# Start addresses of the moving operands: 160 instead of 96 modulo 256, beside weight tiles that stay at 96

## The chip, the cores and the metric

The program runs on one core of a Trainium2 chip. The metric is the device time of one execution in microseconds (us). A core has five engines: TensorE (PE; its weight loads are listed apart as PEld), VectorE (DVE), ScalarE (ACT), GpSimd (POOL) and SyncE (SP, which starts DMAs here).

## What is computed

Two transformer blocks in a row on one sequence of 1024 tokens by 1024 features, all in float32. The first block mixes tokens with three kinds of attention, reads a memory of 256 tokens, and ends with a gated feed-forward network. The second block has a pooling mixer (four groups of 512 features, each averaged over its own window of 2, 4, 8 or 16 tokens) and then a sliding-window attention. Cut to its skeleton:

```python
x = first_block(x, mem, ...)      # attention x3, cross attention, feed-forward, final norm
h = modulate(rmsnorm(x, norm_g[0]), shift, scale)
u, z = split(h @ a_w_in)          # pooling mixer
p = causal_multiscale_pool(u)     # per group: mean over a trailing window, minus u
y = einsum("gc,gcd->gd", p, a_w_group) * a_scale
x = x + gate * ((y * silu(z)) @ a_w_out)
kb, vb = shared_kv_blocks(x, ...)
x = x + gate * swa_sink_mixer(...)   # sliding-window attention
return rmsnorm(x, final_g)
```

Nearly all arithmetic is in dense products `h @ W`.

## The kernel before

**A product in three passes.** Each float32 operand is written as a high part and a low part of type float32r, and a product is the sum of three: high by high, low by high, high by low. `product` (line 681) does this for one strip of weights. The weights are the stationary operand, a slice of 128 by 128 of `split_hi` or `split_lo`; the activations are the moving operand, 128 partitions by 512 columns of `h_hi` and `h_lo` (normed stream), `act_hi` and `act_lo` (hidden layer), `sum_hi` and `sum_lo` (sums of halves), `p_hi`, `p_lo`, `p_lo_x`, `y_hi`, `y_lo` and `pool_sums` (pooling mixer), and some smaller ones. Lines 691, 692 and 694 are its three matmuls. In `product_values` (lines 704 to 706) the sides are changed: a slice of `h_hi` or `h_lo` is stationary and 512 columns of the split weights move. The program issues a weight load ahead of each matmul.

**Weights in strips.** SP loads strips of weights into `raw` (two slots). ACT or POOL rounds them into `split_hi`, POOL subtracts to get `split_lo`, and PE uses them. `split_hi` and `split_lo` have two slots each, so a split waits until PE has done with the slot's last strip.

**Where tiles lie.** `sb` takes the next free bytes of each partition, in the order of the program. `shared` gives a list of tiles the next free bytes one after the other and frees them at once, so that tiles of several `shared` lists lie over each other; padding tiles (`w11`, `w21` and so on) put a tile at a chosen distance. Worked out from the shapes and the order, in bytes of a partition: `raw` begins at 7008, `split_hi` at 15200, `split_lo` at 23392, `h_hi` at 31584, `h_lo` at 64352, `xT` at 97120, and the large shared region at 129888. All of these are 96 modulo 256. Since nearly all later tiles are whole multiples of 256 bytes long, nearly all moving operands start at 96 modulo 256, at each of their 512-column halves too (2048 bytes). I call an operand's start modulo 256 its place, and the difference of the moving operand's place and the weights' place their distance.

**The exception.** `pooled` and `trail` (lines 243 and 244) have rows of T + EDGE floats, EDGE being 16. `w21` and `w22` (2 * EDGE floats, 128 bytes, lines 238 and 241) step over the end of `trail`. So `pool_sums` and `p_lo` begin 128 bytes later than the rest, at place 224. `p_lo_x` (declared behind `w20`) holds other parts of the same low operand and lies at place 96. `pooled_low` (line 600) says which of them a product of the pooling mixer reads: from the second group on, pieces 0 and 1 read `p_lo_x` and pieces 2 and 3 read `p_lo`.

**The other tiles.** `cols`, `cf` (identity and ones), `cb` and the small tiles lie ahead of `raw`. In the attention stages, probabilities, keys, values and queries lie in the shared region; the transposes (line 838) have a piece of probabilities as stationary operand and the identity of `cf` as moving one; line 850 multiplies transposed probabilities (stationary) by values (moving); line 828 makes the scores.

**Order.** The engines run lists written out by hand with semaphores between them. Nothing in the order depends on addresses.

Of the kernel before, what the change touches and what calls it, by code (L numbers as in the profile page):

```python
# [30 lines left out]
F32 = mybir.dt.float32  # L31
F32R = mybir.dt.float32r
# [5 lines left out]
P = 128  # L38
D = 1024
T = 1024  # L40
# [57 lines left out]
EDGE = 16  # L98
# [34 lines left out]
def build(nc, dram, out):  # L133
    ctx = ExitStack()
    with ctx:
# [3 lines left out]
        def sb(name, shape, dt=F32):  # L139
            return ctx.enter_context(nc.sbuf_tensor(name, shape, dt))  # L140

        def shared(tensors):

            with ExitStack() as phase:
                return [phase.enter_context(nc.sbuf_tensor(n, s, d)) for n, s, d in tensors]
# [19 lines left out]
        raw = sb("raw", [P, 2, D])  # L165
        split_hi = sb("split_hi", [P, 2, 8, P], F32R)
        split_lo = sb("split_lo", [P, 2, 8, P], F32R)

        ident, ones = cf[:, C_ID:C_ID + P], cf[:, C_ONE:C_ONE + P]
        eps, eps_squared = cf[:, C_EPS:C_EPS + 1], cf[:, C_EPS + 1:C_EPS + 2]  # L170
# [4 lines left out]
        def col(name, i=0, n=1):  # L175
# [9 lines left out]
        _, p1, pt1 = shared([("mla_qkv", [P, 3 * HEADS, T], F32), ("p1", [P, 4, HALF], F32), ("pt1", [P, 4, HALF], F32)])  # L185
# [3 lines left out]
        _, swa_klo0, swa_bias, p3, pt3 = shared([("x_kept", [P, KEPT, T], F32), ("swa_klo0", [P, T], F32R),  # L189
                                                ("swa_bias", [P, SWA_HEADS, 2 * P], F32), ("p3", [P, 4, 2 * P], F32),  # L190
                                    ("pt3", [P, 4, 2 * P], F32)])
        fox_rows, = shared([("fox_rows", [P, QT, D], F32R)])
        _, memw_lo = shared([("w18", [P, 6, T], F32), ("memw_lo", [P, 2, 8, P], F32R)])
        _, p_lo_x = shared([("w20", [P, 6, T], F32), ("p_lo_x", [P, 2, T], F32R)])
# [9 lines left out]
        _, _, _, _, _, _, fox_norm = shared([  # L204
            ("v1", [P, HEADS, MEM], F32), ("v2", [P, 2, HALF], F32), ("v3", [P, QT, HALF], F32),
            ("v4", [P, HEADS, CHK_SPAN], F32), ("v5", [P, 2, T], BF16), ("v6", [P, T], F32), ("fox_norm", [P, 2, T], F32R)])
        _, _, _, _, _, _, _, _, fox_aug, fox_kr = shared([
            ("a1", [P, HEADS, MEM], F32), ("a2", [P, 2, HALF], F32), ("a3", [P, QT, HALF], F32),
            ("a4", [P, HEADS, CHK_SPAN], F32), ("a5", [P, 2, T], BF16), ("a6", [P, T], F32), ("a7", [P, T], F32), ("a8", [P, T], F32),
            ("fox_aug", [P, HEADS, T], BF16), ("fox_kr", [P, 2, T], F32R)])  # L210
# [6 lines left out]
        _, _, _, memw_hi = shared([  # L217
            ("u1", [P, HEADS, MEM], F32), ("u2", [P, 2, HALF], F32), ("u3", [P, QT, HALF], F32), ("memw_hi", [P, 2, 8, P], F32R)])
# [9 lines left out]
        _, last_hi, last_lo = shared([("w13", [P, 16, T], F32), ("last_hi", [P, HID, T], F32R), ("last_lo", [P, HID, T], F32R)])  # L228
# [2 lines left out]

        _, sq_ffn = shared([("w14", [P, 13, T], F32), ("sq_ffn", [P, T], F32)])
        (_, sq3, sq_sum3, sq4, sq_sum4, rms4) = shared([
            ("w11", [P, 10 * T + 2 * EDGE], F32), ("sq3", [P, T], F32), ("sq_sum3", [P, T], F32),
            ("sq4", [P, T], F32), ("sq_sum4", [P, T], F32), ("rms4", [P, T], F32)])
        _, rms_end = shared([("w15", [P, 20 * T + 2 * EDGE], F32), ("rms_end", [P, T], F32)])
        (p_hi, y_hi, y_lo, _, pool_sums, p_lo) = shared([
            ("p_hi", [P, 4, T], F32R), ("y_hi", [P, 2, T], F32R), ("y_lo", [P, 4, T], F32R), ("w21", [P, 2 * EDGE], F32),
            ("pool_sums", [P, 12, T], F32R), ("p_lo", [P, 2, T], F32R)])
        (last_pair, first_tmp, gates, _, sums_f32, last_tmp) = shared([  # L240
            ("last_pair", [P, 4, T], F32), ("first_tmp", [P, 2, T], F32), ("gates", [P, 4, T], F32), ("w22", [P, 2 * EDGE], F32),
            ("sums_f32", [P, 12, T], F32), ("last_tmp", [P, 2, T], F32)])
        pooled, = shared([("pooled", [P, 4, T + EDGE], F32)])
        _, trail = shared([("w23", [P, 8, T], F32), ("trail", [P, 2, T + EDGE], F32)])
        pool_form = small[:, :, :].rearrange("p a n -> p (a n)")
        _, pool_tmp = shared([("w16", [P, 4, T + EDGE], F32), ("pool_tmp", [P, 3, HALF], F32)])
        _, sq_kv, sq_sum_kv = shared([("w19", [P, 10 * T + 2 * EDGE], F32), ("sq_kv", [P, T], F32), ("sq_sum_kv", [P, T], F32)])
        (swa_stack, swa_q, swa_kv, swa_z, swa_khi, swa_v, osb3, swa_klo1) = shared([
            ("swa_stack", [P, 2, 2, T], F32R), ("swa_q", [P, 2, T], F32), ("swa_kv", [P, 2, T], F32),
            ("swa_z", [P, NK, T], F32), ("swa_khi", [P, 2, T], F32R),  # L250
# [2 lines left out]
        _, gated_early = shared([("w12", [P, 2, 2, T], F32R), ("gated_early", [P, 2, HALF], F32R)])  # L253
# [3385 lines left out]
```

## Time and profile before

| what | value |
|---|---|
| device time, median of 3 runs | 2434.67 us (2433.75 to 2435.26) |
| span of the profiled execution | 2430.9 us |
| PE busy | 2369.3 us, 97% of the span |
| matmuls, weight loads | 11802, 11810 |
| granted TensorE clock, mean | 0.993 |

The profile is one execution, with all engines' instructions. The page gives busy times by engine, a picture of the span in 40 slices, the chain of work that ended last, and the costliest groups of instructions. A matmul's duration in it reaches from its start to the modelled end of its last column, so that successive matmuls overlap; how fast they follow each other is read from their start times. The granted clock has two levels here, 1.2 and 2.4 GHz; 1.00 stands for 2.4.

### The profile page before, as it was taken

How to read it: one execution, taken by the hardware profiler on the slowest of the kernel's cores; microseconds unless marked ns; L12 is line 12 of the kernel's file. 1: busy time of each engine (PE TensorE's matmuls, PEld its weight loads, DVE VectorE, ACT ScalarE, POOL GpSimd, SP SyncE). 2: the span in 40 equal slices, each digit the busy share in tenths (PEclk: the TensorE clock that was granted, in tenths of full speed). 3: DMA queues.
4: the chain of work that ended last, by engine and by line, in shares of the span. 5: the costliest groups of instructions: out<-in, count | busy, mean ns of one | idle time of the engine just before them, and what ended most of it. 6: DMA issues, size and time to landing. Idle time of an engine off the chain costs nothing.

```text
span 2430.9 us, 32848 instructions
## 1 busy us (share of the span) xinstructions
PE 2369.3 (97%) x11802; PEld 1965.9 (81%) x11810; DVE 1510.0 (62%) x1909; ACT 833.6 (34%) x1588; POOL 1273.0 (52%) x724
## 2 busy tenths in 40 slices
PE   7999999999999999999999999999999899999998
PEld 6887788888877888888888878878788787888877
DVE  6725555634577688878887678763754766045555
ACT  4211555612443222222222433231232333055663
POOL 4433964143044666666668344673846633465523
PEclk9999999999999999999999999999999999999999
DMA  5511000021011333333332111121121113100023
GB/s 215 158 44 44 1 1 30 7 113 51 11 40 48 113 120 122 121 121 121 121 121 65 48 44 44 57 65 58 64 82 56 57 64 130 52 27 19 27 101 134
DMA packets 67271, 177.31 MB, mean 73 GB/s; under 512 B 6847, under 2 KB 13761, under 8 KB 65113
## 3 DMA queue, kind: packets, MB, share of 16 engines
q1 hardware_dynamic: 58344, 148.58, 18.1%
q10 hardware_dynamic: 8816, 27.25, 3.2%
q8 instruction: 70, 1.15, 0.2%
q14 instruction: 41, 0.33, 0.0%
HBM read 160.04 MB, written 15.72 MB: 72 GB/s over the span
## 4 chain that ended last, share of the span: by engine, by line
PE 82%; DVE 6%; issue 5%; POOL 4%; ACT 2%; DMA 1%; SPq 0%; DVEq 0%; POOLq 0%; ACTq 0%
PE ps L691 22%; PE ps L694 21%; PE ps L692 21%; PE ps L850 6%; PE ps L828 4%; PE ps L838 3%; POOL split_lo L1606 1%; DVE h_lo L565 1%; PE ps L705 1%; PE ps L704 1%; PE ps L706 1%; PE ps L487 1%; POOL small L1625 1%; DMA raw<-in_strips 1%; DVE h_lo L568 1%
## 5 line engine op out<-in xcount | busy, mean ns | idle before, releaser
L691 PE MATMUL ps<-h_hi,split_hi 128*128 128x512 f32 (+1 forms) x1576 | 628.7, 399 | 20.0 <-DVE h_lo L568 13.3
L692 PE MATMUL ps<-h_lo,split_hi 128*128 128x512 f32 (+1 forms) x1576 | 612.7, 389 | 0.0
L694 PE MATMUL ps<-h_hi,split_lo 128*128 128x512 f32 (+1 forms) x1576 | 548.3, 389 | 0.0
L1482 POOL TENSOR_TENSOR split_hi<-raw,cf 128x1024 fp32r<-128x1024 f32 x70 | 137.0, 1958 | 498.8 <-PE ps L694 393.5
L691 PEld LDWEIGHTS ps<-h_hi,split_hi 128*128 128x128 f32 x1576 | 298.0, 189 | 80.7 <-issue 12.2
L694 PEld LDWEIGHTS ps<-h_hi,split_lo 128*128 128x128 f32 x1576 | 297.3, 189 | 61.8
L692 PEld LDWEIGHTS ps<-h_lo,split_hi 128*128 128x128 f32 x1576 | 298.0, 189 | 56.1 <-issue 1.2
L1557 POOL TENSOR_TENSOR split_lo<-raw,split_hi 128x512 fp32r<-128x512 f32 x144 | 230.4, 1619 | 199.8 <-ACT split_hi L2495 199.5
L1606 POOL TENSOR_TENSOR split_lo<-raw,split_hi 128x512 fp32r<-128x512 f32 x96 | 148.7, 1558 | 170.8 <-ACT split_hi L2653 169.5
L1484 POOL TENSOR_TENSOR split_lo<-raw,split_hi 128x1024 fp32r<-128x1024 f32 x70 | 195.3, 2790 | 5.5
L2495 ACT CAST split_hi<-raw 128x512 fp32r<-128x512 f32 x144 | 86.8, 622 | 286.0 <-PE ps L694 214.0
L888 DVE CUSTOM_DVE_ANT_0 p<-ps,swa_bias 128x256 f32<-128x256 f32 (+1 forms) x128 | 52.2, 408 | 154.1 <-PE ps L828 152.9
L988 ACT COPY pt<-ps 128x256 f32<-128x256 f32 (+3 forms) x216 | 79.9, 370 | 180.9 <-PE ps L838 180.6
L838 PE MATMUL ps<-cf,p 128*128 128x128 f32 x712 | 122.2, 276 | 10.4 <-ACT p L980 6.8
L691 PE MATMUL ps<-act_hi,split_hi 128*128 128x512 f32 x320 | 125.4, 392 | 3.0 <-DVE xT L3131 2.9
L692 PE MATMUL ps<-act_lo,split_hi 128*128 128x512 f32 x320 | 124.5, 389 | 0.0
L2653 ACT CAST split_hi<-raw 128x512 fp32r<-128x512 f32 x96 | 58.7, 621 | 161.9 <-PE ps L694 155.8
L838 PEld LDWEIGHTS ps<-cf,p 128*128 128x128 f32 x712 | 86.8, 144 | 32.8 <-ACT p L980 19.3
L3131 DVE TENSOR_TENSOR xT<-xT,ps 128x1024 f32<-128x1024 f32 x72 | 87.4, 1214 | 31.0 <-PE ps L694 31.0
L3007 DVE SCALAR_TENSOR_TENSOR ada_acc<-ada_raw,cact,ada_acc 128x1024 f32<-128x1024 f32 x56 | 102.6, 1832 | 0.8
L691 PE MATMUL ps<-p_hi,split_hi 128*128 128x512 f32 x256 | 100.1, 391 | 1.5 <-DVE p_lo L3211 1.5
L692 PE MATMUL ps<-y_lo,split_hi 128*128 128x512 f32 x256 | 99.6, 389 | 0.0
(447 smaller groups left out, 5139.7 us busy)
## 6 DMA issues: line engine op xcount, KB each, us to landing
raw<-in_strips SPq DMA_DIRECT2D x208, 256.0 KB, 2.7
raw<-in_strips SPq DMA_DIRECT2D x86, 512.0 KB, 3.5
ada_raw<-in_ada SPq DMA_DIRECT2D x64, 512.0 KB, 3.8
memw_raw<-in_mem_strips SPq DMA_DIRECT2D x8, 512.0 KB, 6.3
xT<-in_xT ACTq DMA_DIRECT2D x4, 1024.0 KB, 7.9
x_spill_d<-xT ACTq DMA_DIRECT2D x1, 3584.0 KB, 9.9
xT<-x_spill_d ACTq DMA_DIRECT2D x2, 1792.0 KB, 11.0
out_T<-out_sb SPq DMA_DIRECT2D x14, 256.0 KB, 2.2
```

Source lines behind the costliest of these rows:

```text
L691: pe.matmul(acc[:, a:b], w_hi, hi[:, a:b], start=first, stop=False)
L692: pe.matmul(acc[:, a:b], w_hi, lo[:, a:b], start=False, stop=False)
L694: mm = pe.matmul(acc[:, a:b], w_lo, hi[:, a:b], start=False, stop=last)
L828: mm = pe.matmul(at[:, lo:hi], q, k, start=j == 0, stop=j == len(group) - 1)
L838: mm = pe.transpose(bank(4 + b % 2, P, j * P), probs[:, (b0 + j) * P:(b0 + j + 1) * P], ident)
L850: mm = pe.matmul(o, a["pt"][:, w % 4, j * P:(j + 1) * P], unit["values"][b0 + j], start=b0 + j == 0, stop=b0 + j == nblk - 1)
L1482: pool.tensor_tensor(hi, raw[:, r, :], ones[:, 0:1].to_broadcast([P, D]), ALU.mult).then_inc(hi_split, 1)
L1484: pool.tensor_tensor(lo, raw[:, r, :], rows(hi), ALU.subtract).then_inc(split_ready[r], 1)
L1557: pool.tensor_tensor(form_tiles(split_lo, p), src, rows(form_tiles(split_hi, p)), ALU.subtract).then_inc(form_ready, 1)
L1606: pool.tensor_tensor(group_tiles(split_lo, p), src, rows(group_tiles(split_hi, p)), ALU.subtract).then_inc(form_ready, 1)
L3007: dve.scalar_tensor_tensor(out=ada_acc[:, :], in0=ada_raw[:, r, :], scalar=cact[:, k:k + 1], in1=ada_acc[:, :], op0=ALU.mult, op1=ALU.add) ...
L3131: dve.tensor_tensor(xT[:, o, :], xT[:, o, :], pair(2 + o % 2), ALU.add).then_inc(ffn_res, 1)
```

## The change

A new tile `beside_weights` of 16 floats (64 bytes) is put behind `split_lo`. It is never used. All tiles behind it begin 64 bytes later: `h_hi`, `h_lo`, `xT` and the large shared region, and with them all moving operands of `product`, which go from place 96 to place 160. `raw`, `split_hi` and `split_lo` stay at 96. The paddings `w21` and `w22` grow from 128 to 256 bytes, and those of the tiles that lie over them likewise, so `pool_sums` and `p_lo` go from place 224 to 160 too. No instruction is added, removed or moved, and no order is changed.

```diff
         split_lo = sb("split_lo", [P, 2, 8, P], F32R)
+        sb("beside_weights", [P, 16])
...
-            ("w11", [P, 10 * T + 2 * EDGE], F32), ("sq3", [P, T], F32), ("sq_sum3", [P, T], F32),
+            ("w11", [P, 10 * T + 4 * EDGE], F32), ("sq3", [P, T], F32), ("sq_sum3", [P, T], F32),
...
-        _, rms_end = shared([("w15", [P, 20 * T + 2 * EDGE], F32), ("rms_end", [P, T], F32)])
+        _, rms_end = shared([("w15", [P, 20 * T + 4 * EDGE], F32), ("rms_end", [P, T], F32)])
...
-            ("p_hi", [P, 4, T], F32R), ("y_hi", [P, 2, T], F32R), ("y_lo", [P, 4, T], F32R), ("w21", [P, 2 * EDGE], F32),
+            ("p_hi", [P, 4, T], F32R), ("y_hi", [P, 2, T], F32R), ("y_lo", [P, 4, T], F32R), ("w21", [P, 4 * EDGE], F32),
             ("pool_sums", [P, 12, T], F32R), ("p_lo", [P, 2, T], F32R)])
...
-            ("last_pair", [P, 4, T], F32), ("first_tmp", [P, 2, T], F32), ("gates", [P, 4, T], F32), ("w22", [P, 2 * EDGE], F32),
+            ("last_pair", [P, 4, T], F32), ("first_tmp", [P, 2, T], F32), ("gates", [P, 4, T], F32), ("w22", [P, 4 * EDGE], F32),
             ("sums_f32", [P, 12, T], F32), ("last_tmp", [P, 2, T], F32)])
...
-        _, sq_kv, sq_sum_kv = shared([("w19", [P, 10 * T + 2 * EDGE], F32), ("sq_kv", [P, T], F32), ("sq_sum_kv", [P, T], F32)])
+        _, sq_kv, sq_sum_kv = shared([("w19", [P, 10 * T + 4 * EDGE], F32), ("sq_kv", [P, T], F32), ("sq_sum_kv", [P, T], F32)])
```

## Rows read from the trace of the kernel before

**Rows 1.** The page: span, engines' busy times, chain that ended last.

```profile
span 2430.9 us, 32848 instructions
...
PE 2369.3 (97%) x11802; PEld 1965.9 (81%) x11810; DVE 1510.0 (62%) x1909; ACT 833.6 (34%) x1588; POOL 1273.0 (52%) x724
...
PE 82%; DVE 6%; issue 5%; POOL 4%; ACT 2%; DMA 1%; SPq 0%; DVEq 0%; POOLq 0%; ACTq 0%
```

**Rows 2.** PE's groups, shapes apart: line, out<-moving,stationary, count | busy us, mean ns | idle.

```profile
L691 PE MATMUL ps<-h_hi,split_hi 128*128 128x512 f32 x1544 | 619.6, 401 | 20.0 <-DVE h_lo L568 13.3 <-DVE h_lo L565 4.7 <-DVE h_lo L2925 1.8
L692 PE MATMUL ps<-h_lo,split_hi 128*128 128x512 f32 x1544 | 603.6, 391 | 0.0
L694 PE MATMUL ps<-h_hi,split_lo 128*128 128x512 f32 x1544 | 539.2, 392 | 0.0
...
L692 PE MATMUL ps<-act_lo,split_hi 128*128 128x512 f32 x320 | 124.5, 389 | 0.0
...
L692 PE MATMUL ps<-y_lo,split_hi 128*128 128x512 f32 x256 | 99.6, 389 | 0.0
...
L691 PE MATMUL ps<-sum_hi,split_hi 128*128 128x512 f32 x240 | 94.4, 393 | 2.1 <-POOL split_lo L1557 2.1
...
L704 PE MATMUL ps<-split_hi,h_hi 128*128 128x512 f32 x64 | 24.9, 389 | 0.0
```

**Rows 3.** One tile's instructions, `p_lo` (224), then `p_lo_x` (96): durations min/median/max ns.

```profile
L692 PE MATMUL ps<-p_lo,split_hi x64: 391/395/395, 1486.6 to 1951.5; 128*128 128x512 f32 x64
...
L692 PE MATMUL ps<-p_lo_x,split_hi x48: 387/389/397, 1633.4 to 1948.7; 128*128 128x512 f32 x48
```

**Rows 4.** One tile's instructions, `pool_sums` (place 224): the three matmul lines.

```profile
L692 PE MATMUL ps<-pool_sums,split_hi x160: 387/393/628, 1483.9 to 1922.6; 128*128 128x512 f32 x160
...
L691 PE MATMUL ps<-pool_sums,split_hi x144: 390/395/792, 1555.5 to 1922.4; 128*128 128x512 f32 x144
...
L694 PE MATMUL ps<-pool_sums,split_lo x144: 390/396/628, 1556.0 to 1922.9; 128*128 128x512 f32 x144
```

**Rows 5.** Timeline of PE, moving operands at 96 only: start us, duration us, instruction.

```profile
1300.10 0.39 PE L691 MATMUL ps<-h_hi,split_hi 128*128 128x512 f32 x1
...
1329.80 0.39 PE L694 MATMUL ps<-sum_hi,split_lo 128*128 128x512 f32 x1
```

**Rows 6.** Timeline of PE, moving operands at 224 only.

```profile
1576.01 0.40 PE L694 MATMUL ps<-pool_sums,split_lo 128*128 128x512 f32 x1
1576.25 0.39 PE L691 MATMUL ps<-pool_sums,split_hi 128*128 128x512 f32 x1
1576.48 0.40 PE L692 MATMUL ps<-pool_sums,split_hi 128*128 128x512 f32 x1
...
1580.92 0.39 PE L694 MATMUL ps<-pool_sums,split_lo 128*128 128x512 f32 x1
```

**Rows 7.** Timeline of PE behind a stall, moving operands at 96.

```profile
1021.26 0.50 PE L691 MATMUL ps<-act_hi,split_hi 128*128 128x512 f32 x1 [0.55 <-DVE xT L3131]
1021.60 0.39 PE L692 MATMUL ps<-act_lo,split_hi 128*128 128x512 f32 x1
...
1022.76 0.39 PE L691 MATMUL ps<-act_hi,split_hi 128*128 128x512 f32 x1
```

**Rows 8.** Timeline of PE, scores of float32 operands, 256 columns each, no float32r.

```profile
611.37 1.02 PE L828 MATMUL ps<-mem_k,cross_q 128*128 128x256 f32 x4
```

**Rows 9.** Timeline of PE at the lower clock; then the groups of the transposes and values.

```profile
761.33 0.63 PE L694 MATMUL ps<-sum_hi,split_lo 128*128 128x512 f32 x1
...
763.46 0.63 PE L692 MATMUL ps<-sum_lo,split_hi 128*128 128x512 f32 x1
...
L838 PE MATMUL ps<-cf,p 128*128 128x128 f32 x712 | 122.2, 276 | 10.4 <-ACT p L980 6.8 <-DVE h_lo L944 2.8 <-DVE small L897 0.3
...
L850 PE MATMUL ps<-vbc,pt 128*128 128x64 f32 x528 | 68.4, 273 | 0.0
```

## What the change does to the time, forecast from these rows

> **What bounds the kernel now.** I read the page first. PE is busy 97% of the span, and the chain of work that ended last lies on PE for 82% of it [rows 1]; each of the three lines of `product` carries some 21 to 22% of the span there. So the kernel is a stream of matmuls, and what counts is how fast one follows the other. The change touches no instruction. It can move the time only if the rate of that stream depends on where the operands lie. So the next views are PE's groups by shape, the single tiles, and the timeline.
>
> In the groups the reader sees one size all over: 512 columns, 389 ns from start to modelled end [rows 2]. The starts tell more. From 1300.10 to 1329.80 us there are 131 matmuls whose moving operand is at place 96, and (1329.80 - 1300.10) / 131 = 226.7 ns from start to start [rows 5]. A duration of 389 ns so goes with a step of 227 ns, 162 ns less. At 2.4 GHz 512 columns take 213.3 ns, if one column goes in per cycle; at the lower clock, 1.2 GHz, (763.46 - 761.33) / 5 = 426 ns is just 512 / 1.2, with nothing on top [rows 9]. So at the higher clock each step has 13.4 ns that the columns don't explain.
>
> **The step does depend on the place.** The pooling mixer's tiles show it. `p_lo` is at 224 and `p_lo_x` at 96; they are pieces of the same operand, read by the same line in the same loop. Their medians are 395 and 389 ns [rows 3], 6 ns apart, and the two ranges (391 to 395; 387 to 397) are narrow. `pool_sums`, also at 224, has medians of 393, 395 and 396 ns [rows 4]. In its unbroken stream, (1580.92 - 1576.01) / 21 = 233.8 ns per step, with single steps of 0.24 and 0.23 us in turn [rows 6]. Against 226.7 that is 7.1 ns more. The weights are at 96 in all of these. So either a distance of 128 bytes to the weights costs 6 to 7 ns, or the place 224 by itself does; the trace can't part the two, as no weights of `product` lie elsewhere. It has no long matmul at place 160, or at a distance of 64, either.
>
> A third fact: at place 96 too the step isn't always 226.7. Behind a stall, five steps from 1021.60 to 1022.76 take 232 ns each [rows 7], before the stream falls into its steady step. So 226.7 is a favourable rhythm that place 96 finds, and some 232 to 234 ns is what it costs to be out of it.
>
> [...]
>
> **The change part by part.** First the tiles that go from 96 to 160. Their matmuls in `product` are: `h_hi` and `h_lo`, 3 x 1544; `act`, 3 x 320; `sum`, 3 x 240; `y_lo`, 256 [rows 2]. `p_hi` has another 512 and `y_hi` 256, and the small ones with `product_values` (3 x 64, where the weights' side moves instead) bring about 400. Together about 7,700. The price of one is unknown, so I bound it. From above, by the nearest rows at another place: 395 - 389 = 6 ns [rows 3], or 7.1 ns by the steady stream [rows 6]. From below, by the smallest excess of any stream in the trace: the scores of rows 8, with float32 operands, start every (1.02 - 0.38) / 3 = 213 to 215 ns (0.38 us being one such matmul's duration) for 256 columns at two cycles each, so nearly no excess. If all 13.4 ns but the 2 of that row were lost through place, a better place could give back 11 ns. So the bounds are -11 and +7 ns. I take +3 ns: the distance, 64 bytes, is halfway between the two that are known (0 costs nothing, 128 costs 6), and place 160 lies halfway between 96 and 224. It is a choice and not a reading. Sum: 7,700 x 3 = 23 us.
>
> Second, the tiles that go from 224 to 160: `pool_sums` 448 and `p_lo` 64 matmuls, 512 [rows 3, 4]. They pay 6 ns now and would pay 3: 512 x -3 = -1.5 us. If the new place were as good as 96, this would be -3 us.
>
> Third, the transposes, 712 with `cf` as the moving side [rows 9], and some 170 more of their kind. Their stationary side moves and the identity stays, so their distance goes from -32 to -96. [...] If each lost the 3 ns, 880 x 3 = 2.6 us, of which part lies beside waits for ACT; I put them at 0 to 2.6 us and take 1. The values (line 850), keys and queries: both sides move by 64, distance as before, nothing from the distance. The other engines' instructions read and write whole rows as before; their durations in the trace don't bear on places, and they have idle time beside PE (DVE 62%, POOL 52% busy [rows 1]), so 0, with up to 1 us either way. DMAs to tiles: `raw` stays; those to `xT` and `ada_raw` are hidden but for the first, 0.
>
> **What of it lies on the path.** PE is idle for 2430.9 - 2369.3 = 61.6 us in all [rows 1], where it waits for splits or norms. Where POOL or ACT end such a wait, slower matmuls just shorten it. The chain has 82% on PE and 5% in issue, and most of the rest is waits that begin with a PE result and so move along. I take 90%: 0.9 x (23 - 1.5 + 1) = 20 us. The sum against the profiled execution: 2430.9 + 20 = 2451; the median of the runs is 3.8 us above the span, so about 2455 us.
>
> **Rivals.**
> 1. *As bad as 224 (slower, in full).* If what counts is which half of 256 bytes a stream begins in, 160 and 224 are alike. Then 7,700 x 6 x 0.9 = 42 us: 2476. For it: 224 is the only other place that is known, and the stream behind a stall also runs at 232 to 234 [rows 6, 7]. Against it: nothing. I treat it as the upper part of my slower case.
> 2. *Nothing happens at 160 (no change).* The good rhythm holds over a window of distances and only 128 falls out. Then the 512 pooled matmuls go from 395 to 389 and 3 us are gained, less if their waits take it up: 2432. For it: 96 and its rhythm are a broad, steady state that returns within some six steps after each stall. Here also belongs the case that place matters for no reason that 64 bytes touch. [...]
> 3. *A better place (faster).* The 13.4 ns are themselves a cost of streams that start at the same place as the weights, and 64 bytes apart they don't meet. The price is per matmul of `product`, and it decides as soon as the step at 160 is under about 226 ns. With half of the 11 ns back: 8,200 x 5.5 = 45 us, or 2390; with all of it 90 us, or 2345. For it: the excess isn't there at 1.2 GHz, nor with float32 operands [rows 8, 9], so it isn't a fixed cost of a matmul. Against it: 0 is the better of the two distances that are known, and the step is the same to 0.1 ns for all 96-tiles, which looks like a floor.
>
> [...]
>
> **How the numbers follow.** A measurement of this kernel can tell about 0.2%, 4.9 us, from no change. Slower by more: 0.46, of which rival 1 takes about half. Within 0.2%: 0.20, rival 2 and small prices. Faster by more: 0.34, rival 3. The likeliest is the slower case, and its time is 2455, its own range 2440 to 2480. The range reaches from half of rival 3's gain, 2385, to rival 1 with a little more, 2482; outside are the full gain of rival 3 and prices above 7 ns, together under 0.2.
>
> **What would show each step.** In the profile after, `h_lo` and `act_lo` on line 692 have a mean duration of 392 ns by my sum (389 now), 395 by rival 1, 389 by rival 2, under 385 by rival 3. An unbroken stream of `h` and `sum` matmuls steps by 230, 233, 227 or under 222 ns. `p_lo` and `p_lo_x` must come out alike, whatever the price; if they don't, place modulo 256 isn't what counts. If the steps stay at 227 and the time moves nevertheless, the cause is outside PE and the whole argument is wrong. The prediction is wrong in its main choice if a place between two known ones isn't between them in price.

## The result: 0.5% slower, and the profile after

The changed kernel takes 2447.85 us (median of 4 runs, 2446.37 to 2449.15) against 2434.97 us of the kernel before on the same chip (4 runs). The ratio is 1.0048, with a 95% interval of 1.0036 to 1.006. The profiled execution's span is 2445.3 us, 14.4 us above that of before.

The page after, its lines that answer to [rows 1]:

```profile
span 2445.3 us, 32848 instructions
...
PE 2382.5 (97%) x11802; PEld 1966.9 (80%) x11810; DVE 1512.1 (62%) x1909; ACT 832.7 (34%) x1588; POOL 1275.5 (52%) x724
...
PE 84%; DVE 7%; issue 4%; POOL 3%; ACT 2%; DMA 1%; SPq 0%; DVEq 0%; POOLq 0%; ACTq 0%
```

The instruction counts are the same. PE is busy 13.2 us longer and idle 62.8 us instead of 61.6, so nearly all of the 14.4 us lies in the stream of matmuls. The other engines' busy times move by at most 2.5 us.

PE's groups after, with shapes apart (lines are one higher, because of the new line of code), answering to [rows 2]:

```profile
L693 PE MATMUL ps<-h_lo,split_hi 128*128 128x512 f32 x1544 | 606.1, 393 | 0.0
...
L693 PE MATMUL ps<-act_lo,split_hi 128*128 128x512 f32 x320 | 125.2, 391 | 0.0
...
L693 PE MATMUL ps<-y_lo,split_hi 128*128 128x512 f32 x256 | 99.9, 390 | 0.0
...
L705 PE MATMUL ps<-split_hi,h_hi 128*128 128x512 f32 x64 | 25.2, 394 | 0.0
```

The mean durations rise by 1 to 2 ns in `product` (`h_lo` 391 to 393, `act_lo` 389 to 391, `y_lo` 389 to 390) and by 5 ns in `product_values` (389 to 394). The single tiles, answering to [rows 3] and [rows 4] (durations min/median/max):

```profile
L693 PE MATMUL ps<-p_lo,split_hi x64: 388/392/394, 1499.4 to 1964.7; 128*128 128x512 f32 x64
```

```profile
L693 PE MATMUL ps<-p_lo_x,split_hi x48: 387/390/397, 1644.4 to 1961.9; 128*128 128x512 f32 x48
```

```profile
L692 PE MATMUL ps<-pool_sums,split_hi x144: 388/392/793, 1568.1 to 1935.3; 128*128 128x512 f32 x144
...
L695 PE MATMUL ps<-pool_sums,split_lo x144: 388/392/628, 1568.6 to 1935.7; 128*128 128x512 f32 x144
```

`p_lo` comes down from 395 to 392 ns and `pool_sums` from 395 and 396 to 392. `p_lo_x`, which left place 96, goes up by 1. Now that all of them are at place 160 they are nearly alike, as they should be if the address modulo 256 is what counts.

The timeline shows the step itself. First a stream of `h` alone, as in [rows 5] (start us, duration us):

```profile
520.28 0.39 PE L692 MATMUL ps<-h_hi,split_hi 128*128 128x512 f32 x1
520.51 0.39 PE L693 MATMUL ps<-h_lo,split_hi 128*128 128x512 f32 x1
520.74 0.39 PE L692 MATMUL ps<-h_hi,split_hi 128*128 128x512 f32 x1
520.97 0.39 PE L693 MATMUL ps<-h_lo,split_hi 128*128 128x512 f32 x1
521.19 0.62 PE L695 MATMUL ps<-h_hi,split_lo 128*128 128x512 f32 x2
```

Successive steps are no longer all 226.7 ns. Read in ns they run 226, 229, 232 and again; from 503.80 to 529.89 us there are 114 steps of 228.9 ns on average. The steady rhythm of [rows 5] is gone, but not the whole price of [rows 6] is paid.

Then a place where this profile holds its own control. Up to 114.11 us `memw` weights and `mem` activations are multiplied; both lie behind the new tile, so both moved and their distance is still 0. From there on line 705 has `h` as stationary side, at 160, and the split weights, at 96, as moving one: distance -64.

```profile
109.81 0.39 PE L707 MATMUL ps<-memw_hi,mem_lo 128*128 128x512 f32 x1
...
113.66 0.39 PE L706 MATMUL ps<-memw_lo,mem_hi 128*128 128x512 f32 x1
113.89 0.39 PE L707 MATMUL ps<-memw_hi,mem_lo 128*128 128x512 f32 x1
114.11 0.39 PE L705 MATMUL ps<-split_hi,h_hi 128*128 128x512 f32 x1
114.35 0.39 PE L706 MATMUL ps<-split_lo,h_hi 128*128 128x512 f32 x1
...
118.78 0.39 PE L707 MATMUL ps<-split_hi,h_lo 128*128 128x512 f32 x1
```

The 19 steps up to 114.11 take (114.11 - 109.81) / 19 = 226 ns, and the 20 steps after it (118.78 - 114.11) / 20 = 233.5 ns. The lines, the shape and the order stay the same across that point, with no idle time; the tiles change, and with them places and distance. Before the change the second group ran like this:

```profile
112.46 0.39 PE L704 MATMUL ps<-split_hi,h_hi 128*128 128x512 f32 x1
...
115.86 0.39 PE L704 MATMUL ps<-split_hi,h_hi 128*128 128x512 f32 x1
```

That is 15 steps of 226.7 ns. Its moving side, the split weights, is at 96 in both kernels, and it lost 6.7 ns all the same; the first group went from 96 to 160 and lost nothing. Both point at the distance and not at the moving operand's place.

Then a stage where the change costs nothing. The sliding-window scores, before and then after (first and last start):

```profile
L828 PE MATMUL ps<-swa_khi,swa_stack x128: 220/364/365, 2130.7 to 2333.1; 128*128 128x256 f32 x112, 128*128 128x128 f32 x16
```

```profile
L829 PE MATMUL ps<-swa_khi,swa_stack x128: 222/364/368, 2143.6 to 2346.0; 128*128 128x256 f32 x112, 128*128 128x128 f32 x16
```

They begin 12.9 us late and end 12.9 us late. In this stage the `product` matmuls come three at a time between others. Where one follows another here, the step was already 229 ns on average before the change and is 229 ns after it: the steady rhythm was never reached, and there was none to lose.

### The profile page after: what moved, and what is told of

Same layout as the page of the kernel before. It is cut to its first block, busy times and chain, and to the rows that moved or that the text cites. A ratio compares the mean times of both kernels' runs of the same rounds, so it can differ in the third digit from the quotient of the medians.

```text
span 2445.3 us, 32848 instructions
## 1 busy us (share of the span) xinstructions
PE 2382.5 (97%) x11802; PEld 1966.9 (80%) x11810; DVE 1512.1 (62%) x1909; ACT 832.7 (34%) x1588; POOL 1275.5 (52%) x724
## 4 chain that ended last, share of the span: by engine, by line
PE 84%; DVE 7%; issue 4%; POOL 3%; ACT 2%; DMA 1%; SPq 0%; DVEq 0%; POOLq 0%; ACTq 0%
PE ps L692 22%; PE ps L695 22%; PE ps L693 22%; PE ps L851 6%; PE ps L829 4%; PE ps L839 3%; POOL split_lo L1607 1%; DVE trail L3228 1%; DVE h_lo L566 1%; PE ps L705 1%; PE ps L707 1%; PE ps L706 1%; PE ps L488 1%; DVE h_lo L569 1%; ACT p L981 0%
```

## The experiments

The question after the result: is it the distance between weights and moving operand that sets the step, or the moving operand's own place? And what does the curve look like? In all kernels below but e9 the paddings `w21` and `w22` have 256 bytes, so that all moving operands of `product` share one place.

### e1: the pooled tiles alone

```diff
-            ("p_hi", ...), ("w21", [P, 2 * EDGE], F32),
+            ("p_hi", ...), ("w21", [P, 4 * EDGE], F32),
```

and the other paddings likewise; no `beside_weights`.

> Only the paddings w21 and w22 (and those over them) grow to 256 bytes; beside_weights is left out. Every moving operand of product, pool_sums and p_lo included, is then at place 96, the weights stay at 96. Theory of the distance and theory of the place agree: 512 matmuls go from 393 to 396 ns down to 389, 3 us less, 2432 us (2429 to 2435). If p_lo stays at 395 ns, something other than address modulo 256 makes these tiles slow.

Measured: 2435.44 us against 2435.56, ratio 1.0001 (0.9992 to 1.001). The matmuls did what both theories say:

```profile
L692 PE MATMUL ps<-p_lo,split_hi x64: 389/389/389, 1489.7 to 1956.1; 128*128 128x512 f32 x64
```

All 64 are at 389 ns, from 395 in [rows 3]. The time didn't follow. The expected gain, 3 us or 0.13%, is just outside the interval. The first and last start of `p_lo` were 464.9 us apart before and are 466.4 here. In e2, e7 and e8 below, where `p_lo` is at distance 0 too, they are 467.6, 463.3 and 463.3 apart. So single executions differ by more than the 3 us that are sought. Matched one by one with those of the kernel before, the 512-column steps without a wait, at the higher clock, take 3.2 us less in e1's trace, but PE's idle time is 64.7 us instead of 61.6. Why it waits longer isn't shown.

### e2: everything 64 bytes later, weights too

```diff
+        sb("ahead_of_weights", [P, 16])
         fox_raw, = shared([("fox_raw", [P, 2, T], F32R)])
```

> The 64 bytes are put ahead of raw instead of behind split_lo, with the larger w21 and w22: weights and moving operands all at place 160, distance 0. Theory A (the distance between weights and moving operand counts): the steady step is 226.7 ns again and the time that of e1, about 2432 us. Theory B (the place of the moving operand counts): place 160 costs as in the changed kernel, steps of 226 to 232 ns, about 2448 us.

Measured: 2436.13 us, ratio 1.0001 (0.9991 to 1.0011). The timeline:

```profile
507.65 0.39 PE L693 MATMUL ps<-h_lo,split_hi 128*128 128x512 f32 x1
...
533.94 0.39 PE L693 MATMUL ps<-h_lo,split_hi 128*128 128x512 f32 x1
```

116 steps, 226.6 ns each. The moving operands are at place 160, just as in the changed kernel, and nothing is lost. The theory of the place falls.

### e3: weights 64 bytes later, moving operands at 96

```diff
+        sb("ahead_of_weights", [P, 16])
         fox_raw, = shared([("fox_raw", [P, 2, T], F32R)])
...
         split_lo = sb("split_lo", [P, 2, 8, P], F32R)
+        sb("beside_weights", [P, 48])
```

> 64 bytes ahead of raw and 192 behind split_lo: weights at place 160, all moving operands at 96, distance -64 (192 modulo 256). Theory A: product costs what lines 705 to 707 cost in the changed kernel, where the distance is -64 and the step 233.3 ns: 7,700 x 6.6 x 0.9 = 46 us more, about 2480 us. Theory B: moving operands are at 96 as before, about 2432 us; only product_values, whose moving side is the weights at 160, changes.

Measured: 2466.94 us, ratio 1.0133 (1.0118 to 1.0149).

```profile
507.76 0.39 PE L693 MATMUL ps<-h_hi,split_hi 128*128 128x512 f32 x1
...
533.90 0.39 PE L693 MATMUL ps<-h_hi,split_hi 128*128 128x512 f32 x1
```

112 steps, 233.4 ns each, though the moving operands are where they were before the change. The distance it is. The step came out as forecast, the time 13 us lower: less than 0.9 of the steps' price reaches the end. The sign counts too: 64 bytes one way cost 2.2 ns, the other way 6.7. The same trace has the mirror image, which the changed kernel has the other way round. In `product_values` the split weights move, so here the distance is +64 where `product` has -64:

```profile
115.01 0.39 PE L706 MATMUL ps<-split_hi,h_hi 128*128 128x512 f32 x1
...
118.90 0.39 PE L708 MATMUL ps<-split_hi,h_lo 128*128 128x512 f32 x1
```

These 17 steps take (118.90 - 115.01) / 17 = 228.8 ns, against 233.4 in `product`. So what counts is the moving operand's start minus the stationary one's, whichever of the two holds the weights.

### e4 to e8, e11, e12: the curve

These differ in the size of `beside_weights` alone (e7: none, but 40 floats ahead of the weights).

```diff
-        sb("beside_weights", [P, 16])
+        sb("beside_weights", [P, 32])
```

> beside_weights has 32 floats (128 bytes) instead of 16: weights at 96, all moving operands of product at 224, distance 128. Theories A and B agree on this one: all of them cost what pool_sums and p_lo cost before, 232.4 to 233.8 ns per step, so 7,700 x 6 x 0.9 = 42 us more, about 2476 us. It tells whether the price of the 512 pooled matmuls holds for all.

> beside_weights has 8 floats: distance 32 bytes, moving operands of product at place 128. If the price rises evenly with the distance from 0 (0: 226.7 ns, 64: 229.0, 128: 232.4), the step is some 228 ns and the time 7,700 x 1.2 x 0.9 = 8 us above before, about 2443 us. Rival: the price is low inside a window around 0 and 32 still falls into the steady rhythm of 226.7 ns: about 2435 us. Rival: a distance just off 0 is better than 0 (the 13 ns above the columns' 213.3 are themselves a cost of meeting): steps of 216 to 224 ns, 2360 to 2420 us.

> beside_weights has 56 floats: distance 224, that is -32 modulo 256; moving operands at place 64. If the curve is even on both sides of 0 it is like e5. If it climbs again to 0 only at the end (192: 233.5), the step is some 230 ns and the time about 2455 us. A step under 226 ns would speak for a best distance other than 0.

> 160 bytes ahead of raw: weights and moving operands all at place 0, distance 0, starts at whole multiples of 256. Theory of the distance alone: 226.7 ns per step, 2435 us as before. Rival: the 13.3 ns above the columns are the price of operands that don't start at a multiple of 128 bytes (17 pieces of 128 bytes are touched instead of 16, and 17 x 13.33 = 226.7): then the step is 213 to 216 ns, and the time 7,700 x 11 x 0.9 = 76 us less, about 2360 us.

> beside_weights has 64 floats: distance 256, which is 0 modulo 256; all places as in e1. If the period is 256 bytes, the step is 226.7 ns and the time that of e1, 2435 us. If what counts is the real distance in bytes or a longer period, as 512, the step is another, 229 to 234 ns, and the time 2447 to 2470 us.

> beside_weights has 24 floats: distance 96, moving operands at place 192. Distances of 32 and 224 cost the most so far and 64 less. If odd multiples of 32 are dear as such, 96 costs 6.2 ns per step, 2470 us. If 64 is the bottom of a dip, with 32 and 128 as its rims, 96 lies between 229.1 and 232.6 ns: 2455 to 2465 us.

> beside_weights has 40 floats: distance 160, moving operands at place 0. Between 128 (232.6 ns) and 192 (233.3): by either reading 233 ns and 2466 to 2471 us. A time under 2455 us would be a second good distance.

Measured, with the step worked out from the same stretch of each timeline, 507.6 to 534.0 us (some 112 to 116 steps; the changed kernel's from 503.80 to 529.89):

| run | distance | step, ns | time, us | ratio to before (95%) |
|---|---|---|---|---|
| e2 | 0 (place 160) | 226.6 | 2436.13 | 1.0001 (0.9991 to 1.0011) |
| e7 | 0 (place 0) | 226.7 | 2431.30 | 0.9994 (0.9984 to 1.0003) |
| e5 | 32 | 233.4 | 2471.08 | 1.0156 (1.014 to 1.0173) |
| changed kernel | 64 | 228.9 | 2447.85 | 1.0048 (1.0036 to 1.006) |
| e11 | 96 | 233.4 | 2470.74 | 1.0156 (1.014 to 1.0172) |
| e4 | 128 | 232.4 | 2465.24 | 1.0125 (1.011 to 1.0141) |
| e12 | 160 | 234.4 | 2476.32 | 1.0176 (1.016 to 1.0192) |
| e3 | 192 (-64) | 233.4 | 2466.94 | 1.0133 (1.0118 to 1.0149) |
| e6 | 224 (-32) | 233.3 | 2470.14 | 1.015 (1.0133 to 1.0168) |
| e8 | 256 | 226.6 | 2431.96 | 0.9996 (0.9984 to 1.0008) |

The ends of three of these stretches, e5, e12 and e7:

```profile
507.62 0.40 PE L693 MATMUL ps<-h_lo,split_hi 128*128 128x512 f32 x1
...
533.99 0.39 PE L692 MATMUL ps<-h_hi,split_hi 128*128 128x512 f32 x1
```

```profile
507.70 0.40 PE L692 MATMUL ps<-h_hi,split_hi 128*128 128x512 f32 x1
...
533.95 0.40 PE L692 MATMUL ps<-h_hi,split_hi 128*128 128x512 f32 x1
```

```profile
507.76 0.39 PE L693 MATMUL ps<-h_lo,split_hi 128*128 128x512 f32 x1
...
533.83 0.39 PE L692 MATMUL ps<-h_hi,split_hi 128*128 128x512 f32 x1
```

In e5 they are 113 steps of 233.4 ns, in e12 112 of 234.4, in e7 115 of 226.7. Starts read to 0.01 us make each step good to 0.1 ns. The stretch is a fair sample: behind their first dozen steps nearly all streams of 36 steps and more in each trace have the step of the table, except at distance 128, where some run at 232.4 ns and some at 233.3.

What follows. Distance 256 is like distance 0, so the pattern repeats after 256 bytes, as far as one such pair can tell. At distance 0 three places (96 in e1 and e8, 160 in e2, 0 in e7) give the same step; in particular, starting at a whole multiple of 256 gives back nothing of the 13 ns that a step has above half of the lower clock's 426 ns [rows 9], the estimate for its 512 columns. And the curve is no smooth hill. It is 226.7 ns at 0, near its full height already 32 bytes away on either side, and among the multiples of 32, the only distances tried, it has one deep dip, at 64. My forecasts for e5 (an even rise, 2443 us; a window, 2435; or a better place, 2360 to 2420) were wrong, and so was 2455 for e6. For e11 the reading that odd multiples of 32 are dear was right to 1 us. For e12 I had expected 233 ns and 2466 to 2471 us, and both came out higher: no reading of mine had distance 160 as the dearest. For e4 the steps were right and the time 11 us too high, as in e3. For e7 and e8 the theories of the distance and of the 256 bytes were right, within 4 us.

The 232.4 to 233.8 ns in e4's forecast are those of the kernel before. Its unbroken streams of `pool_sums` of ten steps and more run at 232.3 to 233.4 ns per step, and 233.8 is the stretch of [rows 6]; the 64 matmuls of `p_lo` are followed by the next one after 233.2 ns on average. One of those streams, 22 steps of 232.3 ns:

```profile
1559.33 0.39 PE L692 MATMUL ps<-pool_sums,split_hi 128*128 128x512 f32 x1
...
1564.44 0.40 PE L694 MATMUL ps<-pool_sums,split_lo 128*128 128x512 f32 x1
```

### e9: the change without the wider paddings

```diff
         split_lo = sb("split_lo", [P, 2, 8, P], F32R)
+        sb("beside_weights", [P, 16])
```

> The change without its larger w21 and w22: beside_weights alone. All moving operands but pool_sums and p_lo are at distance 64 as in the changed kernel; these two are at place 32, distance 192. By the prices found so far (64: 229.1 ns, 192: 233.3) the 512 pooled matmuls cost 4.2 ns each more than in the changed kernel, 2 us: about 2449.5 us against 2447.9. If the pooled stage waits for other engines anyway, as e1 suggests, nothing: 2448 us.

Measured: 2445.13 us against 2432.41, ratio 1.005 (1.0037 to 1.0063), beside 1.0048 for the whole change. The matmuls at distance 192 are slower:

```profile
L693 PE MATMUL ps<-p_lo,split_hi x64: 389/396/399, 1494.0 to 1961.2; 128*128 128x512 f32 x64
```

396 ns in the median against 392 with the wider paddings. This trace also has both distances side by side, `pool_sums` at 192 and then `h` at 64:

```profile
1583.07 0.39 PE L692 MATMUL ps<-pool_sums,split_hi 128*128 128x512 f32 x1
...
1591.23 0.39 PE L695 MATMUL ps<-pool_sums,split_lo 128*128 128x512 f32 x1
```

The 35 steps between these take 233.1 ns each, and the `h` stream from 1591.46 to 1597.87 takes 228.9. In e3 the distance of 192 came from weights at 160 and here from weights at 96; the price is nearly the same. The 2 us that the pooled matmuls should cost can't be told from nothing. So the loss of the change is that of `beside_weights`, and the paddings neither add to it nor take from it measurably.

### e10: only the low weights moved

```diff
+        sb("between_weights", [P, 16])
         split_lo = sb("split_lo", [P, 2, 8, P], F32R)
+        sb("beside_weights", [P, 48])
```

> split_lo alone is put 64 bytes later (place 160, distance -64, price 6.6 ns); split_hi and all moving operands stay at 96. Per piece of weights PE runs lines 691 and 692 twice on split_hi, then 694 twice on split_lo; the load for the next matmul runs while a matmul streams. Theory L (a matmul meets the load of the next one's weights): dear are the second 692, during which split_lo is loaded, and the first 694; the second 694, during which split_hi is loaded, is at 226 to 227 ns. Theory O (a matmul meets its own weights): both 694 are dear and no 692. Either way 2 of 6 are dear: 7,700 / 3 x 6.6 x 0.8 = 13 us, about 2449 us.

Measured: 2454.91 us, ratio 1.0089 (1.0073 to 1.0104). The timeline, two pieces of weights, six matmuls each:

```profile
519.98 0.40 PE L693 MATMUL ps<-h_hi,split_hi 128*128 128x512 f32 x1
520.22 0.39 PE L694 MATMUL ps<-h_lo,split_hi 128*128 128x512 f32 x1
520.45 0.62 PE L696 MATMUL ps<-h_hi,split_lo 128*128 128x512 f32 x2
520.91 0.39 PE L693 MATMUL ps<-h_hi,split_hi 128*128 128x512 f32 x1
521.14 0.40 PE L694 MATMUL ps<-h_lo,split_hi 128*128 128x512 f32 x1
521.37 0.39 PE L693 MATMUL ps<-h_hi,split_hi 128*128 128x512 f32 x1
521.60 0.39 PE L694 MATMUL ps<-h_lo,split_hi 128*128 128x512 f32 x1
521.83 0.63 PE L696 MATMUL ps<-h_hi,split_lo 128*128 128x512 f32 x2
522.29 0.39 PE L693 MATMUL ps<-h_hi,split_hi 128*128 128x512 f32 x1
```

From 520.91 to 522.29 is one piece: 1.38 us for six, 230 ns each. Read in ns, the single steps of this stretch run from 226 to 236 in a pattern that doesn't keep to the six: the dear ones wander from one position of the piece to the next. Averaged over some 700 pieces of this trace, the six positions step by 229, 231, 233, 229, 231 and 232 ns, and none keeps to 226.7. Both theories had two dear matmuls and four at 226.7. The excess is twice what either allows, (231.1 - 226.7) x 6 = 26 ns per piece by the mean step from 507.6 to 534.0 us, instead of 13, and the time is 6 us above the expected 2449. So two distances in turn cost more than their average, and this run doesn't tell whether a matmul meets its own weights' load or the next one's. That stays open.

## Why the prediction came out as it did

**The bound and where the time would move.** Right. PE's busy time took 13.2 of the 14.4 us, nothing else changed.

**The price of a step.** I took +3 ns between bounds of -11 and +7. Measured, 228.9 - 226.7 = 2.2 ns. The mean durations on record for this step, 392 ns from 389, were 391 for `act_lo` and 393 for `h_lo`; the 389 held for `act_lo` alone, as `h_lo` had 391 before [rows 2]. But the reasoning behind the price was wrong. I took the midpoint because 64 lies between 0 and 128. Distance 32 lies between 0 and 64 and costs 6.7 ns. A kernel with half the shift would have been nearly three times as costly, and by the same reasoning I would have forecast the half. The number was right by luck, because 64 happens to be the one deep dip of the curve. The prediction named this as its sign of being wrong, a place between two known ones that isn't between them in price; at 64 it didn't show, and at 32 it does.

**Distance or place.** The prediction left this open and said that no row could part the two. e2 and e3 part them: distance. The section of the trace around 114 us could have parted them already in the profile after, set beside the same section before.

**The sum.** Some 7,720 matmuls x 2.2 ns = 17.0 us. The 192 of `product_values`, at -64, cost 4.4 ns more than I had allowed them at the common price, 0.8 us; I had given both signs of the distance one price. The pooled 512 go from about 233 to 229, -2 us. Together 15.8 us, and the time rose by 12.9: a share of 0.8, where I took 0.9. For the dear distances the share is smaller: in e5, 7,720 x 6.7 = 52 us of steps gave 36.4 us, 0.7. The traces, matched matmul by matmul, say where the rest is. In the changed kernel the 8,089 steps of 512 columns without a wait and at the higher clock took 1850.7 us instead of 1836.9, or 228.8 ns instead of 227.1. That is 13.8 of the span's 14.4 us, so here nearly all of the steps' price reached the end. What was too high is the price times the count: behind stalls, and in the sliding-window stage, the good rhythm wasn't there to be lost [rows 7]. I had seen those rows and didn't take their matmuls off the count. In e5 the same steps took 46.3 us more, not 52, and there waits did take up part of it: PE's idle time fell from 61.6 to 56.5 us. The price and the count account for the forecast of 2455 being 7 us too high.

**The pooled tiles.** The working gave them -1.5 us, and rival 2 gave -3. By e1 and e9 the matmuls do get faster, and the time doesn't show it; the intervals of e7 and e8 leave room for the 3 us.

**The transposes.** The working took 1 us for them. The 712 steps of line 838 took 65.9 us in both traces, so the change of their distance from -32 to -96 cost nothing. The other engines were given 0: in the kernel before, DVE's line 3211 takes 1226 ns in the median to write `p_lo` and `pool_sums` at 224, and 1226 ns in its shortest write of `p_lo_x` at 96.

**The 13 ns above the columns.** The traces give the granted clock as a share: 0.50 from 760.7 to 764.0 us of the kernel before, 1.00 from 1300 to 1330 us. The 1.2 and 2.4 GHz, and with them the 213.3 ns for 512 columns, are my estimate: 512 columns in 426 ns at 0.50 [rows 9] are 1.2 per ns, I took one column per cycle, and half the time at 1.00. Rows 8 show 213 to 215 ns for 256 float32 columns. That this is two cycles for each and so leaves nearly no excess, from which the 11 ns of the lower bound and of rival 3 come, no run shows; what the runs showed in its place is no stream of `product` below 226.6 ns at any distance tried.

**Rival 1** (all that lies away from 96 is as bad as 224) failed for distance 64, and is the rule for all other distances tried. **Rival 2** failed at the step: 228.9 and not 226.7. **Rival 3** failed wholly. No distance and no place brought a step below 226.6 ns. Its strongest reason, that the excess is absent at the lower clock (426 ns for 512 columns) and, by the estimate above, with float32 operands (213 to 215 ns for 256) [rows 8, 9], doesn't make the excess a matter of addresses. What the 13.3 ns are stays unexplained.

**Load and stream.** In the traces a weight load runs while another matmul streams. In e10 a matmul and the load for the next one start together, to 0.01 us, and the load takes 0.19 us of the step of 0.23:

```profile
520.91 0.39 PE L693 MATMUL ps<-h_hi,split_hi 128*128 128x512 f32 x1
520.91 0.19 PEld L694 LDWEIGHTS ps<-h_lo,split_hi 128*128 128x128 f32 x1
521.14 0.40 PE L694 MATMUL ps<-h_lo,split_hi 128*128 128x512 f32 x1
```

Where weights and moving operand lie against each other moves the step from 226.6 to 234.4 ns (e8, e12), and e2 and e3 show that it is their distance. That it is the load and the stream that meet is my reading; e10 was to show it and didn't.

## What to carry to other kernels

In this kernel, where float32r matmuls of 512 columns follow each other with a weight load each, the step was 226.6 to 226.7 ns with weights and moving operands at the same address modulo 256 and 228.9 to 234.4 ns at the other distances tried. A distance of 64 bytes cost 0.5% of the time, the others 1.2 to 1.8%. So in a kernel of this kind try the same address modulo 256 first; no other kernel was measured. Nothing in the order of instructions shows it, so look at start-to-start steps in an unbroken stretch of the timeline. And between two measured addresses don't interpolate: measure the one that is wanted.

## What the runs showed of the chip that I hadn't expected

The step depends on the distance, and at 256 (e8) it is what it is at 0 (e2, e7). The optimum is narrow: 226.6 to 226.7 ns at 0 and 256, 233.3 to 233.4 ns at 32, 96, 192 and 224, 232.4 at 128, 234.4 at 160, and 228.9 at 64. The sign matters, 64 against 192: 228.9 and 233.4 ns. The absolute address doesn't, at the three places tried (226.6 ns at 96 and 160, 226.7 at 0). The step isn't one number but a repeating pattern: 226, 229, 232 ns at distance 64; 229 and 238, or a longer pattern of 228 to 241, at 128 (the kernel before, from 1576.25 us [rows 6] and from 1559.33 us). It settles to a constant step at distance 0 (226 or 227 ns each) and in `product_values` at -64 (233 or 234 ns each, the changed kernel from 114.11 to 118.78 us).
